# Sums of squares in attention: from one full-precision product to two rounded ones

## What is computed

```
q, k, v = split(h @ w_qkv, 3)                  # 8 heads, each with 2 components of 64
q = rms_norm(q.reshape(B, S, 8, 2, 64), q_g)   # x * rsqrt(mean(x*x over 64) + eps) * g
k = rms_norm(k.reshape(B, S, 8, 2, 64), k_g)
logits = q @ k.T / 8 + bias                    # per head and component, causal
p = softmax(logits)
attn = p[component 0] - lam * p[component 1]
o = rms_norm(attn @ v, subln_g) * (1 - lambda_init)
out = o @ w_o
```

## Time and profile before

| | us |
|---|---|
| median of 3 runs | 2626.07 (2625.0 to 2626.41) |
| span of the profiled execution | 2623.0 |
| TensorE products busy | 2579.1 (98%) |
| VectorE busy | 1091.9 (42%) |
| ScalarE busy | 892.4 (34%) |
| GpSimd busy | 999.4 (38%) |

### The profile page before, as it was taken

The page is one execution under the profiler, slowest core; times in us unless marked ns, Lnnn a source line. Parts: engine busy times, 40 slices in busy tenths (PEclk is TensorE's granted clock), DMA queues, the critical chain, the costliest instruction groups (busy, mean ns, idle before and its releaser), DMA issues.

```text
span 2623.0 us, 30510 instructions
## 1 busy us (share of the span) xinstructions
PE 2579.1 (98%) x12706; PEld 2143.0 (82%) x12706; DVE 1091.9 (42%) x1534; ACT 892.4 (34%) x1359; POOL 999.4 (38%) x404
## 2 busy tenths in 40 slices
PE   5999999999999999999999999999999999999999
PEld 5888888776888888888888888888888888888887
DVE  6626254455532325845354353211064555512213
ACT  3222224555422223422224333222252333523324
POOL 2445443221544444445453434444430000444442
PEclk8999999999999999999999999999999999999999
DMA  8645343111433333544443324222232221233232
GB/s 288 204 172 187 128 145 129 65 62 36 136 122 130 127 132 134 191 161 164 152 166 105 97 81 161 96 97 97 85 96 65 65 65 49 83 105 98 90 97 74
DMA packets 249071, 310.54 MB, mean 118 GB/s; under 512 B 7340, under 2 KB 227261, under 8 KB 248934
## 3 DMA queue, kind: packets, MB, share of 16 engines
q1 hardware_dynamic: 246474, 307.04, 34.8%
q10 hardware_dynamic: 2460, 1.56, 0.2%
HBM read 306.46 MB, written 4.74 MB: 119 GB/s over the span
## 4 chain that ended last, share of the span: by engine, by line
PE 94%; DVE 3%; issue 1%; ACT 1%; POOL 0%; DVEq 0%; ACTq 0%
PE bank L1837 21%; PE bank L1832 20%; PE bank L1833 20%; PE bank L1849 5%; PE bank L1850 5%; PE bank L1854 5%; PE bank L1815 2%; PE bank L1760 2%; PE bank L1816 2%; PE bank L1817 2%; PE bank L1864 1%; PE bank L1865 1%; PE bank L1866 1%; PE bank L1677 1%; PE bank L1697 1%
## 5 line engine op out<-in xcount | busy, mean ns | idle before, releaser
L762 POOL TENSOR_TENSOR w_lo_t<-w_raw,w_hi_t 128x1024 fp32r<-128x1024 f32 (+1 forms) x400 | 999.2, 2518 | 1598.6 <-ACT w_hi_t L915 1598.2
L915 ACT CAST w_hi_t<-w_raw 128x1024 fp32r<-128x1024 f32 (+1 forms) x432 | 424.9, 1032 | 695.1 <-PE bank L1837 576.3
L1832 PE MATMUL bank<-h_hi,w_hi_t 128*128 128x512 f32 x1648 | 642.1, 390 | 0.0
L1833 PE MATMUL bank<-h_lo,w_hi_t 128*128 128x512 f32 x1648 | 641.2, 389 | 0.0
L1837 PE MATMUL bank<-h_hi,w_lo_t 128*128 128x512 f32 x1648 | 415.2, 391 | 0.0
L1832 PEld LDWEIGHTS bank<-h_hi,w_hi_t 128*128 128x128 f32 x1648 | 309.4, 188 | 64.3 <-issue 0.5
L1833 PEld LDWEIGHTS bank<-h_lo,w_hi_t 128*128 128x128 f32 x1648 | 309.4, 188 | 64.1 <-issue 0.2
L1837 PEld LDWEIGHTS bank<-h_hi,w_lo_t 128*128 128x128 f32 x1648 | 309.3, 188 | 63.9
L1356 DVE SCALAR_TENSOR_TENSOR scr<-scr,cact 128x1024 f32<-128x1024 f32 x112 | 252.0, 2250 | 75.7 <-DMA scr<-in_ada_w 67.6
L1832 PE MATMUL bank<-act_hi,w_hi_t 128*128 128x512 f32 x720 | 280.3, 389 | 0.3 <-DVE x L1558 0.2
L1833 PE MATMUL bank<-act_lo,w_hi_t 128*128 128x512 f32 x720 | 280.1, 389 | 0.0
(11 more groups left out here) (262 smaller groups left out, 3349.9 us busy)
## 6 DMA issues: line engine op xcount, KB each, us to landing
scr<-in_ada_w SPq DMA_DIRECT2D x128, 512.0 KB, 6.5
w_raw<-in_ffn_wg SPq DMA_DIRECT2D x44, 1024.0 KB, 5.1
w_raw<-in_ffn_wu SPq DMA_DIRECT2D x44, 1024.0 KB, 5.2
w_raw<-in_ffn_wd SPq DMA_DIRECT2D x32, 1024.0 KB, 5.1
w_raw<-in_mlp_w SPq DMA_DIRECT2D x32, 1024.0 KB, 5.4
w_raw<-in_hgrn_w_in SPq DMA_DIRECT2D x16, 1024.0 KB, 5.5
w_raw<-in_ffn_wd SPq DMA_DIRECT2D x16, 768.0 KB, 4.4
w_raw<-in_attn_w_qkv SPq DMA_DIRECT2D x12, 1024.0 KB, 5.2
```

Of the source, the lines that this page charges most:

```text
L762: nc.gpsimd.tensor_tensor(w_lo_t[:, t % 2, k], w_raw[:, t % 2, k], w_hi_t[:, t % 2, k].bitcast(F32), ALU.subtract).then_inc(w_lo, 1)
L915: act.copy(w_hi_t[:, slot, k], w_raw[:, slot, k]).then_inc(w_hi, 1)
L1832: pe.matmul(dst, w, blk(m_hi, kb), start=kb == 0, stop=False)
L1833: pe.matmul(dst, w, blk(m_lo, kb), start=False, stop=False)
```

## The change

The list gets a new step `split`, right behind the second half of each norm unit's product and what `after` put there (the `|` in the example above). In it ScalarE rounds the squares into block 7 of `act_hi`, VectorE takes the remainder into block 7 of `act_lo`, and `ss` then makes two rounded products with a rounded copy of the mask, in place of one in float32. ScalarE waits ahead of its cast until the sum of the unit before is done, since there is one buffer.

```
@@ attn_sequence, unit_done
         if u % 6 < 4:
+            seq.append(("split", u))
             after(1, ("ss", u))
             after(2, ("qk", u))
@@ ScalarE
+                elif step[0] == "split":
+                    j, k = attn_unit(step[1])
+                    n = 4 * j + k
+                    if n == 0:
+                        act.wait_ge(pat_in, 16 * 2)
+                        act.copy(blk64_r[:], blk64[:])
+                    else:
+                        act.wait_ge(qss, n)
+                    act.wait_ge(qsq, n + 1)
+                    act.copy(blk(a_hi_t, 7), sq[:, n % 2, :]).then_inc(qhi, 1)
@@ VectorE
+                if step[0] == "split":
+                    j, k = attn_unit(step[1])
+                    n = 4 * j + k
+                    dve.wait_ge(qhi, n + 1)
+                    dve.tensor_tensor(blk(a_lo_t, 7), sq[:, n % 2, :], blk(a_hi_t, 7).bitcast(F32), ALU.subtract)\
+                       .then_inc(qlo, 1)
@@ TensorE, step "ss"
-                    pe.wait_ge(qsq, n + 1)
+                    pe.wait_ge(qhi, n + 1)
                     if n:
                         pe.wait_ge(qroot, n)
-                    pe.matmul(ps[6][:], blk64[:], sq[:, n % 2, :], start=True, stop=True).then_inc(qss, 1)
+                    pe.matmul(ps[6][:], blk64_r[:], blk(a_hi_t, 7), start=True, stop=False)
+                    pe.wait_ge(qlo, n + 1)
+                    pe.matmul(ps[6][:], blk64_r[:], blk(a_lo_t, 7), start=False, stop=True).then_inc(qss, 1)
```

More of the change, by code:

```diff
@@ L382, in build_program @@
         blk64 = sb("blk64", [P, P])
+        blk64_r = sb("blk64_r", [P, P], F32R)
         ones = sb("ones", [P, P])
@@ L513, in build_program @@
         qsq = sem("qsq")
+        qhi = sem("qhi")
+        qlo = sem("qlo")
         qss = sem("qss")
@@ L1148, in attn_dve @@
             for step in attn_sequence():
-                if step[0] == "qk":
+                if step[0] == "split":
[4 more added lines that the diff above has]
+                       .then_inc(qlo, 1)
+                elif step[0] == "qk":
                     u = step[1]
```

## The result

| | before | after |
|---|---|---|
| median, us | 2626.03 (2625.0 to 2628.2) | 2636.22 (2633.74 to 2636.71) |
| span of the profiled execution, us | 2623.0 | 2634.5 |
| ratio after / before | | 1.0036 [1.0025, 1.0048] |

The change makes the kernel 10.2 us slower. I had forecast 2632.1: the right sign, a size of 6.0 us where 10.2 came, and 0.2 us beyond my range. In the span it is 11.5 us; the profiled execution of after took 2636.51, so 2.0 us lie around its span. My 3.1 for before set the median run against the span of another execution; in the 27 later runs of before it is 1.8 to 2.9 us, mostly about 2. The span of 2623.0 that I worked from is the lowest of those executions too (their median is 2623.9), and that is most of the difference between 10.2 and 11.5.

What follows compares the result with a forecast made beforehand. TensorE was taken to bound the kernel, busy 2579.1 of 2623.0 us. Stalls of 11.7 us (3 x 1.7 + 3 x 2.2) less 5.7 gained gave +6.0 on 2626.1: 2632.1 us, with 8 in 10 from 2619 to 2636.

Steps and rivals of the forecast that it cites:

- The saving on TensorE: At the 16 sums of squares, two rounded products replace a full-precision one: 0.39 us saved per sum, 5.7 us in all.
- The wait between the two products: Between a sum's two rounded products: taken as free; rival, it cancels the saving, 2637.8 us with collisions, 0.07 with anything unseen.
- Units 7, 13, 19: Behind these units the combine's last instruction loses its turn to GpSimd; TensorE stalls 1.7 us each before the row's transposes.
- The margin of 0.02 us: GpSimd arrives 0.02 us before the combine's last instruction; rival, VectorE keeps its turn in both kinds, 2620.4 us, chance 0.15.
- Units 9, 15, 21: Behind these units GpSimd delays the combine, then the norm product; TensorE stalls 2.2 us each before the next heads' first row.
- Units 0 to 3: At the step's start: units 0 and 1 together gain 0.28 us, and rounding at units 2 and 3 costs 0.
- the subtraction of unit 2: On VectorE, beside GpSimd at work: done about 0.2 us ahead of need, cost 0, up to 2 us if caught.
- The lock between VectorE and GpSimd: On SBUF instructions the two block each other fully, 2.83 against 0.69 us; with shared bandwidth instead, about -5 us.

Runs made afterwards that it cites:

- e2: The changed kernel with a 64-column ScalarE copy ahead of each weight conversion in the attention step, so GpSimd starts later: 2621.46 us.
- e1: The changed kernel with VectorE doing the last row's combine ahead of the subtraction at each split step: 2620.33 us.
- e3: The changed kernel with casts and subtractions kept and waited for, but the sum made by one full-precision product: 2641.26 us.
- e5: The changed kernel with the combine put first on VectorE only at units 3, 9, 15 and 21: 2627.87 us.
- e8: The changed kernel without VectorE's subtraction and the second product, the casts kept, so the squares lose their low bits: 2617.00 us.
- e10: e1 with each row's exponentials ahead of the weight conversion on ScalarE: 2621.74 us.
- e4: The changed kernel with idle TensorE products at four places, ahead of unit 1's sum and of the first row of each later pair of heads: 2632.89 us.
- e6: e1 with the sum and norm product of unit 1 one half unit later in the list: 2620.48 us.
- e7: The kernel before the change, with the sum and norm product of unit 1 one half unit later in the list: 2624.88 us.
- e11: e6 with the exponentials ahead of the weight conversion, as in e10: 2620.62 us.

## Why the prediction was right, and where it was short

- **The saving on TensorE: right.** From square to square, units 8 to 9, 14 to 15 and 20 to 21 take 0.40 us less than before, 12 to 13 and 18 to 19 0.47; I had 0.39. The shortest stretches have nothing else in them. The wait between the two products costs nothing.
- **Units 7, 13, 19: right.** 7 to 8, 13 to 14 and 19 to 20 take 1.39 to 1.40 more, against 1.7 - 0.39 = 1.3. The margin of 0.02 us came out as 0.01, which was luck as much as reckoning: e2 shows what a tenth to the other side is worth. Nor had I been sure of the sign, with 0.43 on slower and as much on no change.
- **Units 9, 15, 21: right in the stall, short in what follows.** The stall is 2.0, against 2.2, and the last of them costs 1.70 net, against 1.8. The first two cost 3.19 and 3.21: the stall, and 1.5 more by the clock (3.4 us at half speed are 1.7; some 0.2 of it doesn't show in the time).
- **Units 0 to 3: wrong.** I had -0.67 and +1.59 came. 1.7 of it is the clock behind an idle time that I had right (1.53, and the 0.5 that the sum before it ended earlier), 0.45 the subtraction of unit 2, which GpSimd caught (2.00 us for 0.69) and which I had put at nothing with up to 2 at risk.
- **The term that was missing.** I priced a stall by its own length. Idle TensorE of 1.5 us at the same place had no consequence in the kernel before, and I carried that over to 2.0. The miss of 5.5 us in the span, from square to square: 2.3 at units 0 to 3 (clock and unit 2), 3.0 of clock behind units 9 and 15, 0.65 that was late before the first instruction of the change ran (square of unit 0 at 430.81 against 430.16; over all the runs it lies between 430.06 and 431.47, so this is scatter), less some 0.4 by which the rest came out cheaper. So the step that failed is a term that the sum left at nothing, the clock behind a stall: it took some 4.7 us, 1.7 behind unit 1 and 1.5 behind each of units 9 and 15.
- The lock between VectorE and GpSimd is in the Trainium skill (SBUF — State Buffer, "Who interferes with whom"), and what hung on it holds: 2.92 against 0.75 us. That the issue order decides holds in e2, where VectorE is 0.09 us or more ahead and keeps its turn; nearer than that the starts in a profile don't tell it, since a VectorE instruction that starts 0.01 us ahead loses.

**What stays open.** Not every idle time is followed by half clock. In after, two stalls of 2.0 are and the third isn't; 2.0 ahead of the sum of unit 1 is in after, e1, e2, e3 and e5, and isn't in e8 and e10; in e4 one of 1.6 is; the 1.2 at the step's end is in e5, e6 and e7, and isn't in before, after or e1. I can't say from these runs which ones will be.

Nor is it known for certain how many stretches the unprofiled runs had. Those of after lie at 2633.7 to 2634.4 and 2636.2 to 2636.7; the mean granted clock is 0.993 in the two faster and 0.992 in the four slower, which fits one stretch fewer. e1's profiled execution tells less than it seems: of the 2.1 us by which it lies above its median, 1.3 come behind the last product, where issuing the output's transfer takes 2.28 us against 0.99 in before. Inside the step, from the square of unit 0 to the last square of a head's output, e1's profiled execution takes 213.6 us, e6's 212.3, e11's 212.0 and e10's 211.9. So these three win there, one execution of each. If e1's other runs had no half-clock stretch, that would explain why the medians don't show it, but this isn't shown.

## What to carry to other kernels

Before adding an instruction to an engine's queue, look at what stands behind it and at whom that meets: here the 0.69 us subtraction itself cost 0.45 us at one of its 16 places, and the combine behind it 10.7 us of stalls. Work whose operands are ready belongs ahead of a wait, not behind it; where VectorE and GpSimd work in SBUF side by side, count on a meeting wherever VectorE's start isn't clearly the first (0.09 us was enough here, 0.01 was not), and ask who waits for the result: three meetings of the kernel before cost nothing. And a new stall of TensorE of 1.5 to 2 us is to be priced with up to 1.7 us of clock behind it, each time, as a risk of the range at least.

## What the runs showed of the hardware

- TensorE at 1.2 GHz for some 3.4 us behind idle times of 1.2 us (e5, e6, e7, at the step's end) to 2.05 us, which is 1.7 us of full speed and showed as 1.5 to 1.7 in the time, though not behind each such idle time.
- Between VectorE and GpSimd the turn goes within a tenth of a microsecond: lost at 0.01 behind (534.72 against 534.71), kept at 0.09 and 0.13 ahead. The VectorE instruction that lost ended some 0.5 us behind GpSimd's first half (2.92 us for 0.75).
- A sum in full precision over 512 columns held TensorE some 0.40 us longer than two rounded products (units 8 to 9, before against after).
